# Even and latent attention in steps of four jobs, value products of two heads in column halves

## The reference

```
s   = einsum(q, k) * scale + bias          # causal
p   = softmax(where(mask, s, -1e30)) * mask
o   = einsum(p, v)                         # per head, 64 features
NSA: o = g0 * o_cmp + g1 * o_slc + g2 * o_win,  g = sigmoid(gates)
```

## Time and profile before

| | us |
|---|---|
| median of 3 runs (lowest to highest) | 2254.15 (2251.99 to 2254.44) |
| the profiled execution, its own time | 2254.8 |
| its span | 2253.0 |
| PE busy | 2205.5 |
| DVE busy | 1143.7 |
| ACT busy | 555.1 |
| POOL busy | 1370.2 |

### The profile page before, as it was taken

How to read it: one execution, slowest core, us unless ns; L and a number is a source line. 1 busy time by engine, 2 the same in 40 slices (tenths; PEclk the granted TensorE clock), 3 DMA queues, 4 the chain that set the end, 5 groups by cost and what they waited for, 6 DMA issues and landing times.

```text
span 2253.0 us, 32997 instructions
## 1 busy us (share of the span) xinstructions
PE 2205.5 (98%) x11602; PEld 1865.7 (83%) x11602; DVE 1143.7 (51%) x2318; ACT 555.1 (25%) x1343; POOL 1370.2 (61%) x862
## 2 busy tenths in 40 slices
PE   8999999999999999999999999999999999999997
PEld 6888889778888888888898888888778979888886
DVE  5545304799964574552047544015477546644302
ACT  3111003228742531110030000014356334111000
POOL 6666666681348476666667666656341756666664
PEclk9999999999999999999999999999999999999999
DMA  6433332310133223333323333323221422333331
GB/s 234 152 101 95 94 95 83 133 51 20 48 94 106 66 83 96 100 91 95 96 75 111 98 98 88 102 88 102 71 71 38 122 59 73 100 95 94 94 95 54
DMA packets 62418, 206.14 MB, mean 91 GB/s; under 512 B 6831, under 2 KB 9263, under 8 KB 61924
## 3 DMA queue, kind: packets, MB, share of 16 engines
q1 hardware_dynamic: 55168, 187.79, 27.8%
q10 hardware_dynamic: 7140, 16.90, 2.2%
HBM read 201.98 MB, written 8.70 MB: 94 GB/s over the span
## 4 chain that ended last, share of the span: by engine, by line
PE 89%; DVE 6%; POOL 2%; issue 1%; ACT 1%; DMA 0%; ACTq 0%; POOLq 0%; DVEq 0%
PE bank L813 26%; PE bank L815 26%; PE bank L814 26%; PE bank L1098 3%; PE bank L1081 2%; PE bank L1065 2%; POOL w_lo L655 1%; POOL sq_sum L679 1%; DVE top L2089 1%; DVE ev_logit L1988 1%; PE bank L841 1%; PE bank L1062 1%; PE bank L865 0%; PE bank L1063 0%; DVE sq L2075 0%
## 5 line engine op out<-in xcount | busy, mean ns | idle before, releaser
L655 POOL TENSOR_TENSOR w_lo<-w_raw,w_hi 128x1024 fp32r<-128x1024 f32 (+1 forms) x358 | 864.8, 2416 | 29.9
L813 PE MATMUL bank<-h_hi,w_hi 128*128 128x512 f32 (+1 forms) x2136 | 801.1, 375 | 1.4 <-DVE h_lo L1869 0.9
L653 POOL TENSOR_SCALAR w_hi<-w_raw 128x1024 fp32r<-128x1024 f32 (+1 forms) x358 | 378.2, 1056 | 685.2 <-PE bank L815 517.5
L814 PE MATMUL bank<-h_lo,w_hi 128*128 128x512 f32 (+1 forms) x2136 | 794.2, 372 | 0.0
L815 PE MATMUL bank<-h_hi,w_lo 128*128 128x512 f32 (+1 forms) x2136 | 794.1, 372 | 0.0
L813 PEld LDWEIGHTS bank<-h_hi,w_hi 128*128 128x128 f32 x2136 | 405.9, 190 | 74.4 <-issue 4.0
L815 PEld LDWEIGHTS bank<-h_hi,w_lo 128*128 128x128 f32 x2136 | 405.7, 190 | 69.2
L814 PEld LDWEIGHTS bank<-h_lo,w_hi 128*128 128x128 f32 x2136 | 406.0, 190 | 67.2
L813 PE MATMUL bank<-act_hi,w_hi 128*128 128x512 f32 (+1 forms) x792 | 290.0, 366 | 0.0
L814 PE MATMUL bank<-act_lo,w_hi 128*128 128x512 f32 (+1 forms) x792 | 289.4, 365 | 0.0
L815 PE MATMUL bank<-act_hi,w_lo 128*128 128x512 f32 (+1 forms) x792 | 289.4, 365 | 0.0
(11 more groups left out here) (293 smaller groups left out, 2357.1 us busy)
## 6 DMA issues: line engine op xcount, KB each, us to landing
w_raw<-in_w_up SPq DMA_DIRECT2D x176, 512.0 KB, 3.6
w_raw<-in_w_down SPq DMA_DIRECT2D x64, 448.0 KB, 3.3
w_raw<-in_w_down SPq DMA_DIRECT2D x32, 512.0 KB, 3.5
w_raw<-in_w_ev_in SPq DMA_DIRECT2D x19, 512.0 KB, 3.6
w_raw<-in_w_xkv SPq DMA_DIRECT2D x16, 512.0 KB, 3.6
w_raw<-in_w_od_in SPq DMA_DIRECT2D x16, 512.0 KB, 3.6
bias_line_rows<-bias_lines ACTq DMA_DIRECT2D x1, 6400.0 KB
ev_strip<-bias_line_rows ACTq DMA_DIRECT2D x16, 256.0 KB, 3.0
```

What stands on the lines that cost most here:

```text
L653: pool.tensor_scalar(w_hi[j][:, 0:cols], raw[j][:, 0:cols], 1.0, 0.0, ALU.mult, ALU.add).then_inc(hi_split, 1)
L655: pool.tensor_tensor(w_lo[j][:, 0:cols], raw[j][:, 0:cols], w_hi[j][:, 0:cols].bitcast(F32), ALU.subtract).then_inc(split_done, 1)
L813: pe.matmul(out, w_hi[j][:, w], hi, start=first, stop=False)
L814: pe.matmul(out, w_hi[j][:, w], lo, start=False, stop=False)
```

## The change

- NSA, DSA and MLA run in **groups of four jobs**: two heads (f and f+4 in NSA, neighbours in DSA and MLA) by two tiles (0 and 3, or 1 and 2). The two short jobs share a logit bank, the two long ones have one each; the same for three transposition banks. One group is one step: PE does logits(s), turn(s-2), output(s-3). NSA and DSA are 28 steps, MLA 8.
- The value products take the 64 value columns alone as the stationary operand. Head e writes partitions 64e to 64e+63, and the products of the two heads alternate block by block. The zero padding is gone.
- The compressed branch is one step for its four tiles: eight PE instructions of logits into one bank, eight small drains, one subtraction of the maxima on POOL, one exponential on ACT without row sum, one sum and reciprocal on DVE, two small multiplications on POOL, two transpositions, four value products with 128 stationary rows (`vc` and `vc_odd` hold the values at either tile's rows).
- DVE scales the groups' probabilities as before, after the drains of the next group and with one reciprocal for four jobs.
- POOL has its own order: queries in a ring of eight (`EV_Q`), and the four weight units of the even output projection between them (`EV_W`). The DSA mask products stand behind the three banks' logits.
- MLA's outputs leave in four pieces of 128 partitions, in place of eight of 64. The work on the differential heads is attached to steps 0 to 4.

```diff
...
+Q_TURN, Q_OUT, Q_LEAVE = 2, 3, 4
+QB_LOGIT, QB_TURN = (0, 1, 2), (5, 6, 7)
+N_SETS, SET, Q_RING = 3, 2 * (NT + 1) * P, 8
+EV_Q = {1: 2, 2: 3, 3: 4, 4: 5, 6: 6, 7: 7, 8: 8, 10: 9, 12: 10, 13: 11, 16: 12, 17: 13, 20: 14, 21: 15}
+EV_W = {9: 0, 14: 1, 18: 2, 22: 3}
+OD_W = {2: 0, 4: 1, 5: 2, 6: 3}
...
+def attention_groups():
+
     even = []
     for f in range(A_HEADS // 2):
-        for short in range(NT // 2):
-            for kind, h in (("cmp", f), ("slc", f), ("win", f), ("slc", f + 4), ("win", f + 4)):
-                even += [(kind, h, short), (kind, h, NT - 1 - short)]
-    even += [("dsa", h + e, i) for h in range(0, B_HEADS, 2) for short in range(NT // 2) for e in range(2)
-             for i in (short, NT - 1 - short)]
-    diff = [(f"diff{e}", h, i) for h in range(D_HEADS) for i in range(NT) for e in range(2)]
-    mla = [("mla", h, i) for h in range(C_HEADS) for i in range(NT)]
-    cross = [("x", h, i) for h in range(X_HEADS) for i in range(NT)]
-    return [even, cross, diff, mla, cross]
+        even += [("cmp", f, None)] + [(kind, f, short) for short in range(NT // 2) for kind in ("slc", "win")]
+    even += [("dsa", 4 + p, short) for p in range(B_HEADS // 2) for short in range(NT // 2)]
+    return {0: even, 3: [("mla", p, short) for p in range(C_HEADS // 2) for short in range(NT // 2)]}
...
+    probT_sets = Region(at_sq).put("probT_sets", [P, 2, SET], F32)
...
+    vc_odd = m.put("v_cmp_odd", [P, P], F32)
...
+    def quad_job(kind, f, e, i):
+
+        w, off, tok = P * (i + 1), T - P - P * i, slice(P * i, P * i + P)
+        job = dict(i=i, w=w, tok=tok, rows=slice(DH * e, DH * e + DH), mask=None, k_lo=None, strip=None, gate=None)
+        if kind in ("slc", "win"):
+            b, h, k = ("slc", "win").index(kind), f + 4 * e, 2 * f + e
+            n = 2 * b + e
+            job.update(q=q_st[k % Q_RING][:, tok], k=k_st[n][0][:, 0:w], k_lo=k_st[n][1][:, 0:w], strip=k,
+                       v=[ev_v[:, b, j, DH * e:DH * e + DH] for j in range(i + 1)],
+                       gate=gates[:, i, 3 * h + b + 1:3 * h + b + 2])
+        elif kind == "dsa":
+            k = A_HEADS + 2 * (f - 4) + e
+            job.update(q=q_st[k % Q_RING][:, tok], k=k_st[4][0][:, 0:w], k_lo=k_st[4][1][:, 0:w], strip=k,
+                       v=[ev_v[:, 2, j, 0:DH] for j in range(i + 1)], mask=taken_mask[:, i - 1, 0:w] if i else None)
...
+                g["banks"] = [g["jobs"][0:2], g["jobs"][2:3], g["jobs"][3:4]]
...
+            def scale(phase, s):
+
+                g = GROUPS[phase][s]
+                if g["kind"] == "cmp":
+                    pool.wait_ge(group_coef, g["coef0"] + 1)
+                    rate = gates[:, :, 3 * g["f"]:3 * g["f"] + 13:12]
+                    pool.tensor_tensor(cmp_coef, cmp_coef, rate, ALU.mult).then_inc(cmp_weights, 1)
+                    pool.wait_ge(cmp_weights, g["n"] + 1)
+                    pool.tensor_tensor(cmp_prob[:], cmp_prob[:], cmp_coef.unsqueeze(3).to_broadcast([P, NT, 2, GC]),
+                                       ALU.mult).then_inc(cmp_scaled, 1)
+
+            def cmp_shift(s):
+
+                g = GROUPS[0][s]
+                pool.wait_ge(job_drained, g["drain0"] + 1)
+                pool.tensor_tensor(cmp_prob[:], cmp_logit[:], cmp_max.unsqueeze(3).to_broadcast([P, NT, 2, GC]),
+                                   ALU.subtract).then_inc(cmp_shifted, 1)
+
+            def quad_attention(phase, hooks):
+
+                groups = GROUPS[phase]
+                for s in range(len(groups) + 1):
+                    if s:
+                        scale(phase, s - 1)
+                    if s < len(groups) and groups[s]["kind"] == "cmp":
+                        cmp_shift(s)
+                        pool.wait_ge(cmp_shifted, groups[s]["n"] + 1)
+                    if s in hooks:
+                        if s and groups[s - 1]["kind"] == "cmp":
+                            pool.wait_ge(cmp_scaled, groups[s - 1]["n"] + 1)
+                        hooks[s]()
...
+            quad_attention(0, hooks)
+            units(UNIT["ev_out"], KC, R)
...
+                def logits(s):
+                    g = groups[s]
+                    if g["kind"] == "cmp":
+                        if g["drained"][0]:
+                            pe.wait_ge(job_drained, g["drained"][0])
+                        for i in range(NT):
+                            mm = pe.matmul(bank[QB_LOGIT[0]][:, 2 * GC * i:2 * GC * i + 2 * GC],
+                                           ev[:, QA + g["f"], P * i:P * i + P], kc[:], start=i == 0, stop=i == NT - 1,
+                                           skip_group_check=True)
+                        mm.then_inc(bank_logits, 1)
+                        return
+                    if phase == 0 and g["short"] == 0:
+                        pe.wait_ge(q_lo_done, g["strip"] + 1)
+                        if g["f"] in (0, 4):
+                            pe.wait_ge(k_lo_pool, {"slc": 4, "win": 8, "dsa": 9}[g["kind"]])
+                    if g["kind"] == "dsa" and g["f"] == 4:
+                        pe.wait_ge(mask_done, NT - 1)
+                    masked = []
+                    for b, jobs in enumerate(g["banks"]):
+                        if phase == 3 and s == 0:
+                            k = (QB_LOGIT[b] - CHUNK["ukv"]) % R
+                            pe.wait_ge(q_nope, 4 + 4 + k + 1)
+                            pe.wait_ge(chunk_out, CHUNK["ukv"] + k + 1)
+                        if phase == 3 and s == 1 and b == 0:
+                            pe.wait_ge(q_nope, 4 + 4 + R)
+                            pe.wait_ge(chunk_out, CHUNK["ukv"] + R)
+                        if g["drained"][b]:
+                            pe.wait_ge(job_drained, g["drained"][b])
+                        for n, job in enumerate(jobs):
+                            out = bank[QB_LOGIT[b]][:, job["bank_cols"]]
+                            mm = pe.matmul(out, job["q"], job["k"], start=n == 0, stop=job["k_lo"] is None,
+                                           skip_group_check=True)
+                            if job["k_lo"] is not None:
+                                mm = pe.matmul(out, job["q"], job["k_lo"], start=False, stop=job["mask"] is None,
+                                               skip_group_check=True)
+                        if jobs[0]["mask"] is None and not masked:
+                            mm.then_inc(bank_logits, 1)
+                        else:
+                            masked.append((b, jobs))
+                    for b, jobs in masked:
+                        for job in jobs:
+                            mm = pe.matmul(bank[QB_LOGIT[b]][:, job["bank_cols"]], ident_bf[:], job["mask"], start=False,
+                                           stop=True, skip_group_check=True)
+                        mm.then_inc(bank_logits, 1)
+
+                def turn(s):
+                    g = groups[s]
+                    for b, jobs in enumerate(g["banks"]):
+                        if g["copied0"][b]:
+                            pe.wait_ge(bank_copied[b], g["copied0"][b])
+                        out = bank[QB_TURN[b]]
+                        if g["kind"] == "cmp":
+                            pe.wait_ge(cmp_scaled, g["n"] + 1)
+                            for i in range(0, NT, 2):
+                                mm = pe.transpose(out[:, P * (i // 2):P * (i // 2) + P],
+                                                  cmp_prob[:, i:i + 2, :, :].rearrange("p i g n -> p (i g n)"), ident[:])
+                        for job in jobs:
+                            pe.wait_ge(job_scaled, g["scaled0"] + g["jobs"].index(job) + 1)
+                            for k in range(job["i"] + 1):
+                                to, frm = job["bank_cols"].start + P * k, job["cols"].start + P * k
+                                mm = pe.transpose(out[:, to:to + P], g["set"][:, frm:frm + P], ident[:])
+                        mm.then_inc(bank_turned, 1)
+
+                def output(s):
+                    g = groups[s]
+                    to = bank[B_O[g["f"] % 2]]
+                    if g["opens"] and g["f"] >= 2:
+                        pe.wait_ge(lo_done, SPLIT[OUT_KEY[phase]] + g["f"] - 1)
+                    if phase == 3 and g["opens"] and g["f"] == 1:
+                        pe.wait_ge(sub_normed, D_HEADS)
+                    if g["kind"] == "cmp":
+                        pe.wait_ge(bank_copied[0], g["copied0"][0] + 1)
+                        for i in range(NT):
+                            mm = pe.matmul(to[:, P * i:P * i + P], (vc, vc_odd)[i % 2][:],
+                                           cmp_probT[:, P * (i // 2):P * (i // 2) + P], start=i == 0, stop=False,
+                                           skip_group_check=True)
+                        mm.then_inc(group_out, 1)
+                        return
+                    for at in (0, 2):
+                        pair = g["jobs"][at:at + 2]
+                        if at == 0:
```

(72 more changed lines are left out.)

329 lines of the change are left out of this document (212 added, 117 removed).

## The result

The changed kernel takes 2227.22 us (median of four runs, 2226.84 to 2228.54), the kernel before 2254.3: ratio 0.988, 95% interval 0.987 to 0.989. That is 27 us faster, 8 more than the forecast of 2219 and inside its range. The profiled execution spans 2225.2 us, 27.8 less than before.

A forecast was written before the change was run, and what follows sets the result against it. PE was taken as the bound. NSA and DSA were to go from 139.3 to 114.1 us (-25.2) and MLA from 51.9 to 41.8 (-10.1): 2254.8 - 35.3 = 2219.5, forecast 2219; own range 2209 to 2231, wider range 2209 to 2240.

The forecast's parts named there:

- The bound and the halves: In attention, PE leads; column halves work at once, so a value product costs 0.06 us instead of 0.11.
- change of mode: In each group's value products, switching PE's array mode costs 0.3 us with the way in, an estimate.
- (b): Rival for the value products: the column halves take turns, +32 us, 2251, no change; chance 0.09.
- (c): Rival for the value products: a half's weights do not load beside the other's products, +70 us, 2289; chance 0.05.
- MLA: its total: MLA stage: eight groups of 4.75 us, 1.8 of transpositions and 2 of waits, 41.8 us against 51.9.
- Compressed branch: Compressed branch of each NSA head pair: PE's work falls from 3.0 to 2.0 us, with no change of mode.
- POOL's order: NSA and DSA: weight splits spread between queries hold up DVE's scales, charged 3 us; nobody waits for their transfers.
- slack of 1.5 us: Inside a step, DVE's scale ends some 1.5 us before PE needs it.
- Rival (a): Rival for the attention stages: DVE stands still for all that POOL does, 2239 us; chance 0.15.
- The start: Start of NSA and DSA: first compressed chain and three steps in which PE has only logits, 2.5 us.
- The invert: DVE's reciprocal inside a step: a new wait with two drains behind it, costed at nothing with 0.5 us to spare.
- Small copies and padding: Beside the projection's last chunks: dropped padding zeroing and two more small copies are hidden, otherwise under 1 us either way.

The follow-up runs named there:

- e6: Changed kernel with all value products of the odd head of each pair of jobs left out; 2225.2 us.
- e11: Changed kernel, without gate, with POOL forming the low part of queries 2 to 15 twice; 2235.28 us.
- e9: The gated kernel with queries 2 to 4 also split before the attention starts; 2217.64 us.
- gated kernel: Changed kernel with POOL's side work in NSA and DSA held until PE is at that step's logits; 2216.82 us, and 2216.11 when run again.
- e1: Changed kernel with all value products of one head of a tile pair issued before all of the other's; 2230.41 us.
- e8: The gated kernel with an NSA group first and the compressed branch second in each pair of heads; 2223.09 us.
- e3: Changed kernel, without gate, with queries 2 to 4 split before the attention starts; 2223.22 us.

## Why the prediction was right, and where its steps were off

**The bound and the halves: right, the price partly by luck.** PE led, and the price of the 20 value products decided. e6 shows the halves at work together. 0.06 was taken and 0.055 measured; of the two ends, 0.053 and 0.11, the one from the row halves was the true one. But the 0.06 was taken from the earlier trace rows, which has half as many moving columns (62) and one half of the array alone; at 128 moving columns one half alone costs 0.109 to 0.116 (e6). The number fits because two products share that time, which the earlier trace rows doesn't show. With the change of mode a group costs 1.24 us, not 1.5 (ten pairs of 0.109 are 1.09, so the change costs 0.15 where 0.3 was charged): over 32 groups 8 us in the forecast's favour, which hid other terms that were too small. The cases (b), halves in turn, and (c), weights not beside products, are out: ten products of 0.116 and ten free ones fit neither. The rule cited for (c) does not hold for column halves here.

**MLA: its total right to 0.2 us, by errors that cancel.** One step takes 4.76 us in the timeline (1671.95 to 1676.71), where the forecast had 4.75, but the next two take 5.12 and 5.03, although their value products were 0.26 cheaper than charged.

**Compressed branch: right.** From the timeline it takes 0.94 + 0.31 + 0.82 = 2.07 us per pair, against 2.0.

**POOL's order: the step that failed.** "The weight splits: spread out, and with 1.5 us of slack, I charge 3", and query splits were charged nothing, because nobody waits for them. Asking who waits for POOL's result was the wrong question; who shares its time was the right one. With gate and early queries the stage is 111.9 us, so the collisions that those two take away were worth 120.6 - 111.9 = 8.7 of profiled time, where the forecast had 3 for all. The slack of 1.5 us is smaller than one stall: four scalings of 1.51 become 4.20 or 5.28, because POOL runs two or three queries and a weight unit as a chain.

**Rival (a) had the mechanism, not the size.** Its 2239 us took all of POOL's time as lost to DVE. Measured (e11), of 18 us more POOL 12.3 fell on DVE and 8 on the time. The drains do not stall, as the forecast said: in the changed kernel's timeline the 384-column ones take 0.52 and 0.55 us beside w_lo (at 532.05 and 532.50) and the same with POOL idle (at 536.15 and 536.61).

**The start and the rest of the sum.** Even with the collisions gone, the stage is 111.9 where the forecast without its 3 us for splits has 111.1, although value products were 24 x 0.26 = 6.2 us cheaper than charged. So other terms were 7 us too small, and most of that is in the steps themselves. A middle pair takes 17.9 to 18.1 us where 17.6, less 1.0 for the cheaper value products, was to come. In the one of e9 from 533.26 to 551.38 the four groups' logits take 5.5 us (5.2 charged) and their transpositions 5.6 (4.4 charged), of which 0.53 is a wait for ScalarE's copy. DSA steps take 4.27 to 4.35, where 4.4 less 0.26 was to come. The start was charged at 2.5 and has 1.36 of waiting, 3 us at half clock and the steps without value products; how much of the rest is its own is not settled.

**The invert**, named as the tightest point and costed at nothing, does not show: PE's logits waited for no group's drain in the even stage (the 1.36 us at its start are for the compressed branch's), and for 0.4 us in MLA. Small copies and padding: before its first compressed logits PE waits for the same 0.8 us as in the kernel before.

**What was best.** The gated kernel, 2216 to 2217 us in two sets of runs, beats both: 10 to 11 us under the changed kernel and 38 to 39 under the one before. Some 3 us of this are stretches at the lower clock outside the stage.

## What to carry to other kernels

Two heads with 64-wide values on the two column halves cost what one head costs: look for pairs of narrow stationary operands with the same moving width. Before placing side work on POOL, ask not only who waits for it but which DVE instructions it will stand beside: drains that read PSUM didn't mind here, scalings within SBUF stopped. One semaphore wait that ties POOL's side work to PE's step was worth 7.4 us of a stage of 120.6 where POOL ran in chains, and cost 5.5 of 41.9 where POOL had been early anyway; so gate only stages in which the work would otherwise fall beside the scalings. Before a difference of 1 to 3 us is given to a change, compare the lengths of the stages that it doesn't touch.

## What the runs showed of the hardware that I had not expected

- One column half alone is no quicker than the whole array: 10 products of 64 columns in 1.31 us, 20 whole ones in 2.40, 20 on both halves in 1.31. The gain exists only if the other half has work.
- Products on one half followed by products on the other still overlap for the most part (20 in 1.58 us), though each head's run is issued by itself: later ones on the idle half start before earlier ones on the busy half (the 14th in order is the 17th to start in e1).
- A lengthened scaling ends 0.08 to 0.28 us behind a POOL instruction, by its width, so a chain of POOL instructions can hold four scalings for 5.28 us where 1.51 is their own time.
- 1.36 us of waiting of PE at the start of the stage was followed by 3 us at half clock (granted 0.50 from 504 to 507), which e8, with waits of 0.78 and 1.09 us there, did not have. But the wait alone doesn't settle it: e3, with 1.37 us there and 0.69 a little later, has the clock at 1.00 from 504 to 507, and at 0.50 only from 552.5.
- The same work between the two stages takes 1031.9 us with two stretches at the lower clock, 1033.4 with three and 1035.0 with four.
